# Four feature-major projections per layer in products of 512 columns instead of 256

## The chip, the cores and the metric

The kernel runs on one core of a Trainium2 chip. The metric is the device time of one execution in microseconds (us). The kernel before takes 1752.22 us (median of three runs, 1751.6 to 1752.3).

## The reference

Five stages work on x of 256 tokens by 1024 features, all in float32: two "hybrid" layers (L0, L1), then mixer_ab, cross attention, a convolutional FFN, conformer_conv, cross attention and FFN again. The change is in the hybrid layers only. Cut to what it touches:

```python
h = rms_norm(x, norm_pre)                     # 256 x 1024
proj = h @ w_in                               # sb_q, ml_q, ml_k, xa_q are 512 columns each, among others
z    = einsum(sb_q, sb_k) * d ** -0.5         # stick-breaking attention, 4 heads of 128
q_ml = silu(causal_conv(ml_q, conv_q))        # 4 taps along the tokens
k_ml = silu(causal_conv(ml_k, conv_k))
logits = einsum(xa_q, mem_k)                  # attention over the memory
```

## The kernel before

Every large product is made exactly enough for float32 out of fp32r parts: a weight w and a feature h are each split into a high and a low part, and the product is high w times high h, low w times high h, high w times low h (three passes). ScalarE writes the high parts of the weights (line 583), VectorE the low parts (line 1056), 128x1024 at a time. Such a piece is called a unit (512 KB, loaded by SyncE into a ring of 8 slots). Each engine does its splits at fixed places of its own program: `filled(name, i)` first emits the splits that `for_tile` finds due, which is up to five units beyond the one at which TensorE ends that tile, and only then waits for the tile. `past` does the same with a fixed number of units more. An instruction marked by `link` raises its engine's semaphore, and the engine waits for it before its next one.

A feature-major projection puts 512 output features on the partitions, four tiles f = 0 to 3 of 128 features by 256 tokens. `proj_F` (lines 1722 to 1752) makes them in four units of 2 k-tiles by 512 features, two tiles to a bank, with 96 matmuls of 256 columns. `proj_H` (lines 1754 to 1790) makes two tiles in two units of 4 k-tiles by 256 features. The high and the low part of h lie beside each other in `h_both`, so high w times both is one matmul of 512 columns, and a bank holds one tile: in its left half both products with high h, in its right half high w times low h. VectorE adds the halves (`both`, line 1110, one TENSOR_REDUCE of 128x512 to 128x256). `proj_W` is two `proj_H`. With `staged=True` its first half works in three passes of 256 columns, each waiting for the h tiles that it needs (`features_hi`, `features_lo`). sbk, mk and others already use `proj_W`; sbq, mlq, mlk and xaq use `proj_F`.

The eight PSUM banks go round by the written order `ORDER`: a tile takes the bank that was touched longest ago and is not held. `begin` makes TensorE wait for the mark ("free", ...) of the tile before in that bank. The scores `sbs` 0 to 3 hold their banks until `sbw`, which adds to them.

Order around the change, in each layer. TensorE: hT (transposes of h), sbq, sbk, gate columns mlif, sbv, memT, sbz, (L1: mv), scores sbs, mlq, mlk, sbw, mlv, (L0: mk), mle, mld, the mix sby, mlo, mlz, scores mls, and later xaq, the mix rty, xaz, gmy, scores xas. VectorE: low parts of h (line 1104), sums of sbk, gate rows (lines 1184 to 1203), masks of the scores (lines 1229 and 1230), the convolutions of mlq and mlk (line 1244), sblog (line 1251). ScalarE: high parts of h (line 654), memory norm, copies of sbq (line 690), logs of the scores (lines 733 to 735), first taps (line 743), exps sbw (line 751), copies of mlv (line 753), exps mld (lines 764 and 765).

Of the kernel before, what the change touches and what calls it, by code (L numbers as in the profile page):

```python
# [8 lines left out]
ACT = mybir.ActivationFunctionType  # L9
ALU = mybir.AluOpType  # L10
# [98 lines left out]
def build(nc, A, out, known):  # L109
# [5 lines left out]
    with ctx:  # L115
# [57 lines left out]
        def feat(i, n=1):  # L173
            return sec(i, n).rearrange("p (j s) -> p j s", s=S)
# [4 lines left out]
        def rows_of(i, n=2):  # L179
            return sec(i, n).rearrange("p (t n) -> p t n", t=NT)  # L180
# [26 lines left out]
        def two(*names):  # L207
            return [(n, i) for n in names for i in range(2)]

        def four(*names):  # L210
            return [(n, i) for n in names for i in range(4)]

        def pick(name, *at):
            return [(name, i) for i in at]
# [14 lines left out]
        GATES = lambda b: two(f"yT{b}") + four(f"gate{b}", f"up{b}")  # L229
        ORDER = {}  # L230
        for l in range(DEPTH):
            ORDER[f"L{l}"] = ((pick("cols", 0) if l == 0 else four("mk")) + four("hT") + two("sbq") + (pick("cols", 1) if l == 0 else []) + four("sbk") + pick("mlif", 0)
                              + two("sbv") + four("memT") + two("sbz") + (two("mv") if l else []) + four("sbs") + two("mlq", "mlk") + four("sbw") + two("mlv")
                              + (four("mk") if l == 0 else []) + pick("mle", 0) + four("mld") + two("sby", "mlo", "mlz")
                              + (two("mv", "cols2") if l == 0 else []) + four("mls") + two("rtq", "rtk") + four("mly")
                              + two("rtv", "rtz", "gmu", "gmv", "rqT", "rkT", "gmz") + four("rts")
                              + pick("wsT", 0) + two("xaq", "rty", "xaz", "gmy") + four("xas") + GATES(0) + four("xap")
                              + GATES(1) + two("xay") + GATES(2) + GATES(3) + two("yT4") + four("gate4", "up4") + pick("mgT", 0, 1) + pick("o", 0, 1) + pick("mgT", 2, 3) + pick("o", 2, 3))
            ORDER[f"X{l}"] = (pick("v", 2, 3) + four("hT", "q") + pick("q", 4, 5) + pick("s", 0, 1) + pick("q", 6, 7) + pick("p", 0, 1) + pick("s", 2, 3) + pick("oT", 0, 1)
                              + pick("p", 2, 3) + pick("o", 0, 1) + pick("oT", 2, 3) + pick("o", 2, 3))  # L240
            ORDER[f"F{l}"] = ((pick("k", 0, 1) if l == 0 else []) + four("hT") + (pick("k", 2, 3) if l == 0 else []) + four("o")
                              + [g for j in range(6) for g in four(f"g{j}", f"u{j}")])
# [43 lines left out]
        def halves(b):  # L286
            return b[:, :].rearrange("p (j s) -> p j s", j=2)
# [5 lines left out]
        def weight_order():  # L293
# [29 lines left out]
            def win(l, *at):  # L323
                for c in at:
                    col("w_in", (l,), c)
# [5 lines left out]
            for l in range(DEPTH):  # L331
                mem_k, mem_v = (lambda: halved("w_mem_kv", (l,), 0)), (lambda: col("w_mem_kv", (l,), W))
                if l:
                    mem_k()
                win(l, SBQ)
                halved("w_in", (l,), SBK)
                got.append((True, kmaj("w_in", (l,))[:, :, MLI:MLI + 2 * H]))
                win(l, SBV, SBZ)
                if l:
                    mem_v()  # L340
                win(l, MLQ, MLK, MLV)
                if l == 0:
                    mem_k()
                win(l, MLO, MLZ)
                if l == 0:
                    mem_v()
                win(l, RTQ, RTK, RTV, RTZ, GMU, GMV, GMZ)
                plain(A["gm_ws"][l].rearrange("g p q -> p g q"))
                win(l, XAQ, XAZ)
                for b in range(5):  # L350
                    win(l, GATE + b * D, GATE + b * D + W)
                    chunk("w_up", (l, b), 0)
                crossed("w_out", (l,))
# [215 lines left out]
        def _(act):  # L569
            def link(ins, *names):  # L570
                ins.then_inc(act_done, SC(*names))
                act.wait_ge(act_done, SC.n)
# [95 lines left out]
            def layer(l):  # L668
# [16 lines left out]
                if l == 0:  # L685
                    up_to(8)
                    act.wait_ge(mem_in, 16)
                    whole_norm(rows_of(6), "mem", loaded=True)
                for i in range(2):
                    copy(feat(0)[:, 2 * i:2 * i + 2, :], "sbq", i, ACT.Copy, f"sbq{i}", view=halves, scale=HD ** -0.5)  # L690
                if l == 0:
                    copy(cols[:, 8:104], "cols", 1, ACT.Copy, "cols", view=lambda b: b[:, 8:104])
                for_tile("sbk", 3)
# [41 lines left out]
                    link(nc.scalar.activation(e, e, ACT.Ln, bias=1.0), f"sbln{h}")  # L735

                def taps(n, name, s):
                    for i in range(2):
                        b = halves(filled(name, i))
                        for j in range(2):  # L740
                            ft = 2 * i + j
                            c = 52 * l + 16 + 16 * n + 12 + ft
                            link(nc.scalar.activation(feat(s)[:, ft, :], b[:, j, :], ACT.Copy, scale=cols[:, c:c + 1]),
                                 f"{name}.tap{ft}")

                taps(0, "mlq", 11)
                taps(1, "mlk", 12)
# [61 lines left out]
                for t in range(NT):  # L809
                    copy(tok(21)[:, t, :], "gmz", t, ACT.Silu, f"gmz{t}")  # L810
                head_norm("rt")
                for i in range(2):
                    copy(feat(2)[:, 2 * i:2 * i + 2, :], "xaq", i, ACT.Copy, f"xaq{i}", view=halves)
                for t in range(NT):
                    copy(tok(17)[:, t, :], "xaz", t, ACT.Silu, f"xaz{t}")
                pr = sec(15, 2)
# [224 lines left out]
        def _(dve):  # L1041
# [127 lines left out]
            def layer(l):  # L1169
# [8 lines left out]
                    all_of(feat(4), "mk", (2, 3), 2)  # L1178
                if l == 0:
                    whole_norm(rows_of(6), rows_of(6), "mem", "mem.n")  # L1180
                all_of(feat(1), "sbk", range(4), 4)
                b = filled("mlif")
                dve.wait_ge(bif_in, 4 * 16)
# [46 lines left out]
                    link(tt(e, e, con(C_LKM, TRI), ALU.mult), f"sblk{h}")  # L1230

                def conv(n, name, s):
                    for i in range(2):
                        b = halves(filled(name, i))
                        for j in range(2):
                            ft = 2 * i + j
                            dve.wait_ge(act_done, after_act(f"{name}.tap{ft | 1}"))
                            for d in range(1, 4):
                                c = 52 * l + 16 + 16 * n + 4 * (3 - d) + ft
                                y = feat(s)[:, ft, d:S]  # L1240
                                marks = [("free", name, i)] if d == 3 and j == 1 else []
                                if marks and i == 1:
                                    marks.append(name + ".conv")
                                link(stt(y, b[:, j, 0:S - d], cols[:, c:c + 1], y, ALU.mult, ALU.add), *marks)

                conv(0, "mlq", 11)
                conv(1, "mlk", 12)
# [78 lines left out]
                        link(tt(tok(20)[:, t, :], tok(20)[:, t, :], brow[:, o:o + W], op), *(["gmln"] if t and op == ALU.add else []))  # L1326
                b = quarters(filled("wsT"))
                link(tt(wsT[:, :, :], b, con(C_GMM).unsqueeze(1).to_broadcast([P, 4, P]), ALU.mult), "wsT", ("free", "wsT", 0))
                for t in range(NT):
                    b = filled("rty", t)  # L1330
                    link(nc.vector.tensor_copy(tok(22)[:, t, :], b[:, :]), ("free", "rty", t))
# [293 lines left out]
        def _(pe):  # L1625
# [219 lines left out]
            def layer(l):  # L1845
# [12 lines left out]
                norm_T()  # L1858
                if l:
                    proj_H("mk", 1, M_HL["L1"], (1,))  # L1860
                proj_F("sbq", **NORMED)
                if l == 0:
                    pe.wait_ge(rows_in, 10 * 16)
                    b = begin("cols", 1)
# [13 lines left out]
                proj_T("sbz")  # L1878
                if l:
                    proj_T("mv", src=M_HL["L1"])  # L1880
                pe.wait_ge(act_done, SC.at("sbq1"))
                pe.wait_ge(vec_done, VC.at("sbksum3"))
                for h in range(H):
                    scores("sbs", h, feat(0), feat(1))
                proj_F("mlq")
                proj_F("mlk")
                sbr = sec(13, 2)
                for h in range(H):

# [73 lines left out]
                for g in range(4):  # L1963
                    ins = nc.tensor.transpose(b[:, g, :], w[:, g, :], ident)
                used(ins, ("wsT", 0))
                proj_F("xaq")
                pe.wait_ge(vec_done, VC.at("rtsc3"))
                for t in range(NT):
                    mix("rty", t, sbr, tok(6))
# [3 lines left out]
                for t in range(NT):  # L1973
# [1 line left out]
                    for g in range(4):  # L1975
                        ins = mm(b[:, g, :], wsT[:, g, :], tok4(20)[:, t, g, :], start=True, stop=True)
                    end(ins, "gmy", t)
                pe.wait_ge(act_done, SC.at("xaq1"))
                for h in range(H):
                    b = halves(begin("xas", h))  # L1980
                    for t in range(NT):
# [292 lines left out]
```

## Time and profile before

| | |
|---|---|
| median of three runs | 1752.22 us |
| span of the profiled execution | 1750.3 us |
| TensorE busy | 1740.1 us, 99% |
| VectorE busy | 1283.1 us, 73% |
| ScalarE busy | 1024.5 us, 59% |
| matmuls | 9406 |
| share of the chain that ended last | TensorE 91%, VectorE 6% |

The profile gives the span of its execution, from the first to the last instruction, and no time beside it; the timed runs lie 1.3 to 2.0 us above the span. A busy time of TensorE counts matmuls from start to modelled end, so its pace is read better from the starts of groups in the timeline than from the mean of one.

### The profile page before, as it was taken

The page shows a single profiled execution, that of the slowest core. Times are in us where ns is not written, and L with a number is a line of the kernel's source. Part 1 is how long each engine was busy: PE and PEld are TensorE (multiplying, and loading weights), DVE is VectorE, ACT ScalarE, POOL GpSimd, SP SyncE. Part 2 cuts the span into 40 slices and gives each one's busy share as a digit, 9 for nine tenths or more (in the row PEclk, how much of TensorE's full clock was granted, in tenths as well). Part 3 has the DMA queues.
Part 4 walks back from the last instruction along what each step waited for, and adds up shares of the span by engine and source line. Part 5 has one row for each costly group of instructions (what it writes and reads, how often), then busy time and mean ns, then how long its engine had stood idle before and what let it go on. Part 6 is the DMA issues. An engine that isn't in the chain of part 4 may idle for free.

```text
span 1750.3 us, 24767 instructions
## 1 busy us (share of the span) xinstructions
PE 1740.1 (99%) x9406; PEld 1512.0 (86%) x9406; DVE 1283.1 (73%) x1714; ACT 1024.5 (59%) x1417; POOL 114.3 (7%) x186
## 2 busy tenths in 40 slices
PE   9999999999999999999999999999999999999998
PEld 8988898888889888888889988888888988888887
DVE  6966676665877586757669787688778987678775
ACT  7865566454666655644555765755556656555544
POOL 5000000000000000000000000500003360000000
PEclk9999999999999999999999999999999999999999
DMA  9656654566765566565666664456665515356663
GB/s 303 193 157 178 177 169 151 175 190 186 213 181 160 166 181 175 156 181 169 191 195 197 182 192 157 144 182 193 192 186 186 171 36 181 121 169 188 188 189 109
DMA packets 204070, 306.64 MB, mean 175 GB/s; under 512 B 12362, under 2 KB 100340, under 8 KB 203824
## 3 DMA queue, kind: packets, MB, share of 16 engines
q1 hardware_dynamic: 201056, 298.91, 56.1%
q0 software_dynamic: 2896, 6.15, 1.1%
q8 instruction: 75, 1.23, 0.3%
q14 instruction: 43, 0.35, 0.1%
HBM read 303.97 MB, written 1.05 MB: 174 GB/s over the span
## 4 chain that ended last, share of the span: by engine, by line
PE 91%; DVE 6%; ACT 1%; issue 1%; DMA 0%; DVEq 0%; ACTq 0%
PE bank L1696 52%; PE bank L1761 22%; PE bank L1728 8%; DVE bank L1573 2%; DVE weights_lo L1056 2%; PE bank L1801 1%; PE bank L1815 1%; PE bank L2093 1%; PE bank L2111 1%; PE bank L1823 1%; PE bank L1784 1%; ACT weights_hi L583 1%; PE bank L2017 0%; PE bank L1982 0%; PE bank L2065 0%
## 5 line engine op out<-in xcount | busy, mean ns | idle before, releaser
L1056 DVE TENSOR_TENSOR weights_lo<-weights_raw,weights_hi 128x1024 fp32r<-128x1024 f32 x560 | 668.9, 1233 | 248.6 <-ACT weights_hi L583 243.7
L583 ACT ACTIVATE weights_hi<-weights_raw 128x1024 fp32r<-128x1024 f32 x560 | 574.8, 1056 | 386.0 <-DMA weights_raw<-in_w_in_dram 181.3
L1696 PE MATMUL bank<-weights_hi,h_parts 128*128 128x512 f32 x1856 | 567.6, 391 | 0.4 <-DVE h_parts L1478 0.2
L1696 PEld LDWEIGHTS bank<-weights_hi,h_parts 128*128 128x128 f32 x1856 | 348.1, 188 | 73.3 <-DVE h_parts L1478 0.6
L1696 PE MATMUL bank<-weights_lo,h_parts 128*128 128x512 f32 x928 | 348.0, 390 | 0.0
L1696 PE MATMUL bank<-weights_hi,arena_parts 128*128 128x512 f32 x928 | 270.1, 391 | 0.0
L1761 PE MATMUL bank<-h_parts,weights_hi 128*128 128x512 f32 (+1 forms) x992 | 241.0, 385 | 0.5 <-DVE arena L1110 0.4
L1696 PEld LDWEIGHTS bank<-weights_lo,h_parts 128*128 128x128 f32 x928 | 174.4, 188 | 35.3
L1696 PEld LDWEIGHTS bank<-weights_hi,arena_parts 128*128 128x128 f32 x928 | 173.6, 188 | 35.4
L1761 PEld LDWEIGHTS bank<-h_parts,weights_hi 128*128 128x128 f32 x992 | 175.3, 189 | 31.8 <-DVE arena L1110 0.9
L1696 PE MATMUL bank<-weights_lo,arena_parts 128*128 128x512 f32 x464 | 158.4, 390 | 0.0
L1110 DVE TENSOR_REDUCE arena<-bank 128x256 f32<-128x512 f32 x148 | 102.1, 690 | 66.3 <-PE bank L1761 63.4
L1761 PEld LDWEIGHTS bank<-h_parts,weights_lo 128*128 128x128 f32 x992 | 134.8, 191 | 8.8
L1761 PE MATMUL bank<-h_parts,weights_lo 128*128 128x256 f32 x992 | 138.4, 283 | 0.0
L1728 PE MATMUL bank<-h_parts,weights_hi 128*128 128x256 f32 x768 | 133.7, 284 | 0.0
L1728 PEld LDWEIGHTS bank<-h_parts,weights_hi 128*128 128x128 f32 x768 | 116.3, 192 | 0.2 <-issue 0.2
L1696 PEld LDWEIGHTS bank<-weights_lo,arena_parts 128*128 128x128 f32 x464 | 87.2, 188 | 17.9
L1728 PE MATMUL bank<-h_parts,weights_lo 128*128 128x256 f32 x384 | 99.8, 284 | 0.0
L603 ACT ACTIVATE arena<-bank 128x512 f32<-128x512 f32 x140 | 83.0, 593 | 15.4 <-PE bank L1696 9.0
L1728 PEld LDWEIGHTS bank<-h_parts,weights_lo 128*128 128x128 f32 x384 | 69.7, 192 | 0.2 <-DVE weights_lo L1056 0.2
L960 ACT ACTIVATE arena<-arena,vector_columns 128x256 f32<-128x256 f32 x48 | 28.9, 602 | 64.7 <-DVE arena L1110 64.7
L541 POOL TENSOR_SCALAR arena<-constants_sb,vector_columns 128x128 f32<-128x128 f32 x76 | 35.4, 486 | 390.0 <-PE bank L1696 207.5
(326 smaller groups left out, 1667.6 us busy)
## 6 DMA issues: line engine op xcount, KB each, us to landing
weights_raw<-in_w_in_dram SPq DMA_DIRECT2D x224, 512.0 KB, 3.7
weights_raw<-in_f_w_up_dram SPq DMA_DIRECT2D x96, 512.0 KB, 3.5
weights_raw<-in_f_w_down_dram SPq DMA_DIRECT2D x48, 512.0 KB, 3.6
weights_raw<-in_w_up_dram SPq DMA_DIRECT2D x40, 512.0 KB, 3.5
weights_raw<-in_c_w_pw_dram SPq DMA_DIRECT2D x24, 512.0 KB, 3.6
weights_raw<-in_ab_w_in_dram SPq DMA_DIRECT2D x20, 512.0 KB, 3.8
weights_raw<-in_w_mem_kv_dram SPq DMA_DIRECT2D x16, 512.0 KB, 3.6
weights_raw<-in_w_out_dram SPq DMA_DIRECT2D x16, 512.0 KB, 3.6
```

The costliest lines, as they stand in the source:

```text
L541: ins = nc.gpsimd.tensor_scalar(diag(ft, d), ident, cols2[:, c:c + 1], 1.0, ALU.mult, ALU.mult)
L583: nc.scalar.activation(w_hi[:, q % SPLIT, 0:w], raw[:, n % RAW, 0:w], ACT.Copy).then_inc(hi_done, 1)
L603: link(nc.scalar.activation(dst, (view(b) if view else b[:, :]), func, **kw), ("free", name, i), *marks)
L960: link(nc.scalar.activation(c[:, f, :], feat(2)[:, f, :], ACT.Identity, scale=cols2[:, w0 + 48 + ft:w0 + 49 + ft], bias=cols2[:, b0 + ft:b ...
L1056: tt(w_lo[:, n % RAW, 0:w], raw[:, n % RAW, 0:w], w_hi[:, q % SPLIT, 0:w].bitcast(F32), ALU.subtract)\
L1110: link(nc.vector.tensor_reduce(dst, b, AX.X, ALU.add), ("free", name, f), f"{name}sum{f}")
L1573: stt(dst, feat(2, 2)[:, ft, 0:S - d], cols2[:, c:c + 1], acc[:, j, d:S], ALU.mult, ALU.add)\
L1696: return mm(bs[t][:, :], sp_[:, 2 * u + kk, t * P:(t + 1) * P], wp[:, kk, :], start=first and u == us[0] and kk == 0 and n == 0, stop=last ...
L1728: return mm(bs[i][:, j, :], wp[:, kk, f * P:(f + 1) * P], sp_[:, 2 * u + kk, :], start=first and u == us[0] and kk == 0 and n == 0 and j == 0,
L1761: return mm(out, w[n][:, kk, j * P:(j + 1) * P], sp_, start=u == 0 and kk == 0 and n == 0, stop=u == 1 and kk == 3, skip_group_check=True)
L1784: ins = mm(bs[j][:, 1, :], w[0][:, kk, j * P:(j + 1) * P], src[1][:, k, :], start=False, stop=u == 1 and kk == 3, skip_group_check=True)
L1801: ins = nc.tensor.transpose(b[:, j, t * P:(t + 1) * P], src[:, t, (2 * i + j) * P:(2 * i + j + 1) * P], ident)
```

## The change

sbq, mlq, mlk and xaq are made by `proj_W` instead of `proj_F` (sbq with `staged=True`). Their weights are loaded in halves of 256 features, each tile has its own bank, and VectorE adds the halves of the banks. For sbq ScalarE first writes the scaled left half and VectorE adds the scaled right half to it. For mlq and mlk VectorE's sums go to SBUF (`feat(s - 2)`), from where ScalarE makes the first tap and VectorE the other three. For xaq the sums go to `feat(2)` and ScalarE's copies are gone.

```diff
-ORDER: two("sbq") ... two("mlq", "mlk") ... two("xaq", "rty", "xaz", "gmy")
+ORDER: four("sbq") ... four("mlq") + four("mlk") ... four("xaq") + two("rty", "xaz", "gmy")
 # weight order
-                win(l, SBQ)
+                halved("w_in", (l,), SBQ)
...
-                win(l, MLQ, MLK, MLV)
+                halved("w_in", (l,), MLQ)
+                halved("w_in", (l,), MLK)
+                win(l, MLV)
...
-                win(l, XAQ, XAZ)
+                halved("w_in", (l,), XAQ)
+                win(l, XAZ)
 # ScalarE
-                for i in range(2):
-                    copy(feat(0)[:, 2 * i:2 * i + 2, :], "sbq", i, ACT.Copy, f"sbq{i}", view=halves, scale=HD ** -0.5)
+                for f in range(4):
+                    b = filled("sbq", f)
+                    link(nc.scalar.activation(feat(0)[:, f, :], b[:, 0:S], ACT.Copy, scale=HD ** -0.5), f"sbq.part{f}")
 def taps(n, name, s):
-                        b = halves(filled(name, i))
...
+                    for ft in range(4):
+                        for_tile(name, ft)
+                        act.wait_ge(vec_done, after_vec(f"{name}sum{ft}"))
+                        c = 52 * l + 16 + 16 * n + 12 + ft
+                        link(nc.scalar.activation(feat(s)[:, ft, :], feat(s - 2)[:, ft, :], ACT.Copy, scale=cols[:, c:c + 1]),
+                             f"{name}.tap{ft}")
...
-                for i in range(2):
-                    copy(feat(2)[:, 2 * i:2 * i + 2, :], "xaq", i, ACT.Copy, f"xaq{i}", view=halves)
 # VectorE, ahead of sbk's sums
+                for f in range(4):
+                    b = filled("sbq", f, 4)
+                    dve.wait_ge(act_done, after_act(f"sbq.part{f}"))
+                    link(stt(feat(0)[:, f, :], b[:, S:2 * S], HD ** -0.5, feat(0)[:, f, :], ALU.mult, ALU.add), ("free", "sbq", f), f"sbq{f}")
 def conv(n, name, s):
+                    all_of(feat(s - 2), name, range(4), 4)
+                    for ft in range(4):
+                        dve.wait_ge(act_done, after_act(f"{name}.tap{ft}"))
...
 # VectorE, ahead of the copies of rty
+                all_of(feat(2), "xaq", range(4), 4)
 # TensorE
-                proj_F("sbq", **NORMED)
+                proj_W("sbq", staged=True)
...
-                proj_F("mlq")
-                proj_F("mlk")
+                proj_W("mlq")
+                proj_W("mlk")
...
-                proj_F("xaq")
+                proj_W("xaq")
```

The scores now wait for VectorE's marks sbq3 and xaqsum3 instead of ScalarE's sbq1 and xaq1. By `ORDER`, the banks of mlk 0 to 3 are now those of mlq 0 to 3, and the banks of mlv 0 and 1 are those of mlk 0 and 1.

## Rows read from the trace of the kernel before

**Rows 1.** The page: span; busy us, share, instructions; TensorE's granted clock in 40 slices.

```profile
span 1750.3 us, 24767 instructions
...
PE 1740.1 (99%) x9406; PEld 1512.0 (86%) x9406; DVE 1283.1 (73%) x1714; ACT 1024.5 (59%) x1417; POOL 114.3 (7%) x186
...
PEclk9999999999999999999999999999999999999999
```

**Rows 2.** TensorE's waits: us in total, times, longest us.

```profile
PE bank L1843 <- DVE arena L1172: 1.2, 1, 1.2
PE bank L1801 <- DVE arena L1089: 0.8, 1, 0.8
```

**Rows 3.** Timeline of TensorE, layer 1: start us, length us, instruction, count.

```profile
474.62 1.12 PE L1728 MATMUL bank<-h_parts,weights_hi 128*128 128x256 f32 x8
...
486.13 2.00 PE L1761 MATMUL bank<-h_parts,weights_hi 128*128 128x512 f32 x8
...
497.31 0.28 PE L1870 MATMUL bank<-h_parts,weights_hi 128*100 128x256 f32 x1
```

**Rows 4.** Timeline of all engines, 5 to 36 us, layer 0's first projection.

```profile
9.12 1.97 ACT L654 ACTIVATE h_parts<-bank,vector_columns 128x256 fp32r<-128x256 f32 x4
...
9.72 1.19 PE L1728 MATMUL bank<-h_parts,weights_hi 128*128 128x256 f32 x8
...
14.05 0.96 ACT L654 ACTIVATE h_parts<-bank,vector_columns 128x256 fp32r<-128x256 f32 x2
...
15.85 1.00 DVE L1104 SCALAR_TENSOR_TENSOR h_parts<-bank,vector_columns,h_parts 128x256 fp32r<-128x256 f32 x2
...
21.59 0.25 PE L1865 MATMUL bank<-constants_sb,vector_rows 104*128 104x104 f32 x1
```

**Rows 5.** Groups by form, VectorE: busy us, mean ns of one, idle before.

```profile
L1110 DVE TENSOR_REDUCE arena<-bank 128x256 f32<-128x512 f32 x148 | 102.1, 690 | 66.3 <-PE bank L1761 63.4
...
L1534 DVE SCALAR_TENSOR_TENSOR arena<-arena,vector_columns 128x255 f32<-128x255 f32 x48 | 23.2, 484 | 2.0 <-DVE arena L1110 0.4
```

**Rows 6.** Timelines of VectorE, ScalarE and TensorE, layer 0, 34 to 100 us.

```profile
39.40 0.47 DVE L1184 TENSOR_SCALAR arena<-bank,gate_biases 4x256 f32<-4x256 f32 x1
...
70.07 0.56 DVE L1230 TENSOR_TENSOR arena<-arena,constants_sb 128x384 f32<-128x384 f32 x1
70.67 4.63 DVE L1056 TENSOR_TENSOR weights_lo<-weights_raw,weights_hi 128x1024 fp32r<-128x1024 f32 x4
...
45.56 1.21 ACT L603 ACTIVATE arena<-bank 128x512 f32<-128x512 f32 x2
...
68.85 0.53 ACT L735 ACTIVATE arena<-arena 128x384 f32<-128x384 f32 x1
...
60.85 0.36 PE L1728 MATMUL bank<-h_parts,weights_hi 128*128 128x256 f32 x1
```

**Rows 7.** Timelines of VectorE, ScalarE and TensorE, layer 1, 520 to 590 us.

```profile
544.74 0.56 DVE L1230 TENSOR_TENSOR arena<-arena,constants_sb 128x384 f32<-128x384 f32 x1
...
560.72 6.16 DVE L1244 SCALAR_TENSOR_TENSOR arena<-bank,vector_columns,arena 128x255 f32<-128x255 f32 x12
566.91 2.33 DVE L1251 SCALAR_TENSOR_TENSOR arena<-bank,constants_sb 128x384 f32<-128x384 f32 x4
...
544.08 3.90 ACT L583 ACTIVATE weights_hi<-weights_raw 128x1024 fp32r<-128x1024 f32 x4
...
574.02 0.58 ACT L603 ACTIVATE arena<-bank 128x512 f32<-128x512 f32 x1
...
537.17 0.36 PE L1728 MATMUL bank<-h_parts,weights_hi 128*128 128x256 f32 x1
...
560.29 0.60 PE L1893 MATMUL bank<-arena,constants_sb 128*128 128x256 f32 x2
...
563.72 0.47 PE L1696 MATMUL bank<-weights_hi,h_parts 128*128 128x512 f32 x1
...
577.54 0.39 PE L1835 MATMUL bank<-arena 128*128 128x128 f32 x2
```

More of the change, by code:

```diff
@@ L231, in build @@
         for l in range(DEPTH):
-            ORDER[f"L{l}"] = ((pick("cols", 0) if l == 0 else four("mk")) + four("hT") + two("sbq") + (pick("cols", 1) if l == 0 else []) + four("sbk") + pick("mlif", 0)
-                              + two("sbv") + four("memT") + two("sbz") + (two("mv") if l else []) + four("sbs") + two("mlq", "mlk") + four("sbw") + two("mlv")
+            ORDER[f"L{l}"] = ((pick("cols", 0) if l == 0 else four("mk")) + four("hT") + four("sbq") + (pick("cols", 1) if l == 0 else []) + four("sbk") + pick("mlif", 0)
+                              + two("sbv") + four("memT") + two("sbz") + (two("mv") if l else []) + four("sbs") + four("mlq") + four("mlk") + four("sbw") + two("mlv")
                               + (four("mk") if l == 0 else []) + pick("mle", 0) + four("mld") + two("sby", "mlo", "mlz")
@@ L236, in build @@
                               + two("rtv", "rtz", "gmu", "gmv", "rqT", "rkT", "gmz") + four("rts")
-                              + pick("wsT", 0) + two("xaq", "rty", "xaz", "gmy") + four("xas") + GATES(0) + four("xap")
+                              + pick("wsT", 0) + four("xaq") + two("rty", "xaz", "gmy") + four("xas") + GATES(0) + four("xap")
                               + GATES(1) + two("xay") + GATES(2) + GATES(3) + two("yT4") + four("gate4", "up4") + pick("mgT", 0, 1) + pick("o", 0, 1) + pick("mgT", 2, 3) + pick("o", 2, 3))
@@ L737, in taps @@
                 def taps(n, name, s):
-                    for i in range(2):
-                        b = halves(filled(name, i))
[L740 to L744, printed above, removed]
+                    for ft in range(4):
[4 more added lines that the diff above has]
+                             f"{name}.tap{ft}")
                 taps(0, "mlq", 11)
@@ L811, in layer @@
                 head_norm("rt")
-                for i in range(2):
-                    copy(feat(2)[:, 2 * i:2 * i + 2, :], "xaq", i, ACT.Copy, f"xaq{i}", view=halves)
                 for t in range(NT):
@@ L1232, in conv @@
                 def conv(n, name, s):
[L1233 to L1244, printed above, removed]
+                    all_of(feat(s - 2), name, range(4), 4)
+                    for ft in range(4):
+                        dve.wait_ge(act_done, after_act(f"{name}.tap{ft}"))
+                        for d in range(1, 4):
+                            c = 52 * l + 16 + 16 * n + 4 * (3 - d) + ft
+                            y = feat(s)[:, ft, d:S]
+                            link(stt(y, feat(s - 2)[:, ft, 0:S - d], cols[:, c:c + 1], y, ALU.mult, ALU.add),
+                                 *([name + ".conv"] if d == 3 and ft == 3 else []))
                 conv(0, "mlq", 11)
@@ L1880, in layer @@
                     proj_T("mv", src=M_HL["L1"])
-                pe.wait_ge(act_done, SC.at("sbq1"))
+                pe.wait_ge(vec_done, VC.at("sbq3"))
                 pe.wait_ge(vec_done, VC.at("sbksum3"))
@@ L1977, in layer @@
                     end(ins, "gmy", t)
-                pe.wait_ge(act_done, SC.at("xaq1"))
+                pe.wait_ge(vec_done, VC.at("xaqsum3"))
                 for h in range(H):
```

## The prediction

> **What bounds the kernel now.** I read the page's busy times first, then TensorE's waits, then timelines of the stretches that the change touches, one engine at a time, and the groups of instructions by form for the prices. TensorE is busy for 1740.1 of the span's 1750.3 us [rows 1], and its longest waits are 1.2 us, at the very start, and 0.8 [rows 2]. So each microsecond less of matmul stream is a microsecond less of time, and each new wait of TensorE is a microsecond more. The profiled execution has the span 1750.3 us; the timed runs' median is 1752.22, 1.9 us above it. I add to the span and keep the 1.9.
>
> **The stream of products.** An old projection (96 products of 256 columns) runs from 474.62 to 486.13, 11.51 us, and the form it is to take (32 products of 512 columns, 32 of 256) is already there for sbk: 486.13 to 497.31, 11.18 us [rows 3]. One changed projection is worth 0.33 us; for sbq only the second half takes the wide form, 0.165. That is 6 x 0.33 + 2 x 0.165 = 2.3 us over two layers, if nothing waits. By pace: 0.120 us per narrow product before, and 2.79 us per weight unit after against 2.88.
>
> The Trainium skill, TensorE: Matmul & The Clock Gate, section Back-to-back issue gap, gives a warm gap of N/2.4 + 2.5 ns. By it the old form is 96 x 109 ns and the new one 32 x 216 + 32 x 109, and a projection gains 0.08 us, the eight 0.6. Here a narrow product takes 120 ns, so the sum goes by the rows.
>
> **What is added and removed elsewhere.** Per layer VectorE gets 12 sums of a bank's halves at 0.69 us [rows 5] and 4 scalar_tensor_tensor of 256 columns at 0.50 [rows 4], some 10.6 us with gaps, and ScalarE loses two copies of xaq. The convolution's 12 instructions cost VectorE 6.16 us as before (they now read SBUF and not a bank; the same instruction with both operands in SBUF is 0.484 us elsewhere [rows 5], so no gain and no loss, 0.51 with the gap [rows 7]). The same 512 KB per unit is loaded, in other slices, at no cost that I can see: sbk's form arrives no later. What matters is who stands in line behind the new sums. TensorE starts a pair of tiles only when the last readers of both their banks are done; ScalarE and VectorE work in program order, with weight splits in between (0.98 and 1.15 us each, four before mlq's first tile before, now two before each pair of tiles).
>
> **Layer 0, sbq.** The staged form takes the h tiles twice as fast: its first unit wants tiles 0 to 3, its second 4 to 7. ScalarE makes 0 to 3 by 11.09 and, behind two splits, tiles 6 and 7 at 14.05 to 15.01; VectorE's low parts of these end at 16.85 [rows 4]. First unit: high pass ends 11.4, two passes of 0.96 follow, 13.4. Second: its last high tile is at 15.0, so the pass ends 15.35, the weights' low pass 16.3, then two products, a wait to 16.95 and six more: 17.7. The other two tiles take 5.59: 23.3 against 21.6 now: **+1.7 us**. In layer 1 all eight tiles are made by 475.4, h low by 476.9, no wait is left, and it gains 0.165.
>
> VectorE in layer 0 now does four instructions and waits for ScalarE's four parts of sbq, which wait for the memory norm, before sbk's sums. I make that sums from 32.85 instead of 30.71, so the gate rows start at 41.6 instead of 39.40 and ScalarE's string that begins with the sbv copies at 45.56 starts 2.2 us late; it runs without a hole to the last log of the scores at 69.38, so it arrives 2.2 late [rows 6].
>
> **The hand-over from mlq to mlk.** Scores hold four banks until sbw. Before, mlq's two and mlk's two tiles filled the other four. Now mlq takes all four, and mlk's first pair needs the banks of mlq 0 and 1, free when VectorE has summed them. VectorE comes to it after the last mask product of the scores (70.07 + 0.56) and two of the four splits that followed. Layer 0: 70.67 + 2.33 + 1.42 = 74.42, plus the 2.2: 76.6, restart 76.7. TensorE would be there at 60.85 + 1.7 + 11.18 = 73.7: a gap of 3.0 us. Where it began mlk at 72.4 (half of the 23.12 us that both took in layer 1), it now begins 4.3 late [rows 6]. Layer 1, in the old trace's times: 545.34 + 2.33 + 1.42 = 549.07 against 537.17 + 11.18 = 548.35: a gap of 0.8 with the restart at 549.15 [rows 7]. mlk's second pair is just in time in both (sums 2 and 3 end 554.5, needed 554.74).
>
> **From mlk to the mix, layer 1.** VectorE: convolution of mlq 554.5 to 560.7, two splits to 563.0, mlk's sums 0 and 1 to 564.45, two splits behind ScalarE's to 568.4, sums 2 and 3 to 569.8, convolution to 576.0, four sblog to 578.35. Before, sblog ended at 569.24 [rows 7]: 9.1 us late now, of which 5.7 are the eight sums and the rest is waiting for splits and taps in turn. TensorE: mlk ends 560.33, sbw (3.43 us) 563.77, then mlv needs mlk's banks 0 and 1: 564.55, a gap of 0.8. mlv, mle and mld end about 578.3 (mlv 11.0 us), the weights sbw3 come from ScalarE at 578.95. The second mix tile writes the bank of mlv 0, which ScalarE empties only after its exps and four splits: 578.95 + 3.93 + 0.6 = 583.5. TensorE is there at 579.95: a gap of 3.6. It began at 577.54; it now begins at 583.55, **+6.0** including two projections' 0.66. No later tile waits that I can find: mlo's banks are free by 585.1.
>
> Layer 0 has the mk projection of 11.2 us between mlv and the mix, which covers the late exps. There mlv waits for mlk's sum 1, at 89.75 + 2.2 by the same string, so mlv begins 92.05 instead of 87.40 (60.85 and the 26.55 us from mlq to mlv of layer 1): **+4.65** in all, the 1.7 of sbq and both projections in it. mk's second half needs ScalarE's split at about 107.5, 1 us before TensorE; the mix has 0.3 us to spare at mk's sum 2.
>
> **xaq.** The sums stand just before VectorE's rty copies, which wait for TensorE anyway, and xas comes the whole xaz projection of 11 us later. Hidden; -0.33 each. Without that cover the four sums would cost up to 2.8 us per layer.
>
> Sum: 4.65 - 0.33 + (-0.17 + 6.0 - 0.33) = **+9.8 us**. Span 1760.1, time **1762.0**. Bounds: if layer 0's string is late only by what TensorE itself is (1.7) 0.5 less; if a restart costs 0.3 instead of 0.1 at five places, 1 more; the splits' waits in the string, 1.5 either way.
>
> **Rivals.** (a) The new sums hide, as VectorE is idle for a quarter of the span [rows 1]: only the stream counts, 1752.2 - 2.3 = 1749.9, faster. For it: sbk, in this form, waits for nothing now. Against: sbk has a bank rotation of eight, mlk has four, and VectorE is in line behind the masks with its splits [rows 6].  Its mark is that mlk's first product follows mlq's last within 0.3 us in both layers. (b) ScalarE's lateness does not reach the mix (its splits are done while it waits, say): layer 1 loses its two gaps of 0.8 and gains 0.8, layer 0 is some 3 to 4 late: +4, 1756.2. With VectorE one split earlier at the hand-overs, as little as +2.5, 1754.7, no measurable change. (c) The gaps of 3.0 and 3.6 us let TensorE's clock fall. In this trace the granted clock is at its full level throughout [rows 1] and no wait is longer than 1.2 us [rows 2], so no row shows it; a unit of 2.79 us at 1.2 GHz instead of 2.4 would take as much again. One unit at each of the two gaps is +5.6: 1767.6. The Trainium skill, same page, section Why this matters for your kernels, asks for no gaps of that order between bursts of matmuls; by that rule (c) holds. (d) The change does not do what it says, the wide form costing as much as the narrow: 2.3 more than the forecast, 1764.3; against it stand the two rows of sbk and sbq side by side.
>
> **Chances.** Forecast with (d) 0.70 (1759 to 1765), (b) 0.14, half of it within 0.2%, (c) 0.09, (a) 0.07. A change of 0.2% (3.5 us) is about what a measurement of this kernel tells from none: faster 0.06, same 0.10, slower 0.84. The range reaches to (b) and (c): 1755.5 to 1768.
>
> **What would show it.** TensorE's list of waits gets four new entries of 0.7 to 3.7 us: at mlk's first product in both layers (for VectorE's sums), at mlv's (the same), and at the mix tile of layer 1 (for ScalarE's copy of mlv), where the long one stands. A staged sbq in layer 0 ends near 17.7 and sbk begins near 23.3. Unstaged projections of the changed kind take 11.18 us. VectorE's last sblog of layer 1 ends some 9 us later against the scores. If mlk follows mlq without a gap the forecast is wrong at its centre; if the mix tile doesn't wait, it is wrong by 3.6 us.

## The result and the profile after

The changed kernel takes 1758.93 us (median of four, 1758.83 to 1759.32), the kernel before 1752.01 beside it (1751.6 to 1752.3): 6.9 us more, ratio 1.0040 (95% interval 1.0026 to 1.0054). It is slower, and by less than the 9.8 us forecast: 1758.93 lies in the forecast's range of 1755.5 to 1768, and just below the 1759 at which its own narrower interval begins.

The page: span, busy us, granted clock.

```profile
span 1757.1 us, 24388 instructions
...
PE 1740.7 (99%) x9182; PEld 1501.2 (85%) x9182; DVE 1302.5 (74%) x1746; ACT 1023.1 (58%) x1417; POOL 116.2 (7%) x186
...
PEclk9999999999999999999999999999999999999999
```

TensorE's busy time is 0.6 us more than before [rows 1], though there is 2 us less of stream: among others, matmuls at a lower clock, of which more below, count as busy. Most of the 6.8 us of span stands in the list of TensorE's waits (us in total, times, longest), against [rows 2]:

```profile
PE bank L1837 <- ACT arena L606: 3.1, 1, 3.1
PE bank L1698 <- DVE arena L1341: 2.4, 2, 1.2
PE bank L1845 <- DVE arena L1173: 1.2, 1, 1.2
PE bank L1763 <- ACT h_parts L657: 1.0, 2, 0.5
PE bank L1803 <- DVE arena L1090: 0.8, 1, 0.8
```

Three are new: the second mix tile of layer 1 waits for ScalarE's copy of mlv (3.1), the first gate tile of each layer for the VectorE instructions that read gmy out of its bank (1.2 each), and sbq of layer 0 for its h tiles (0.5 twice).

TensorE, layer 0 (start, length): the staged sbq from 10.12, sbk from 23.73, mlq from 62.95, mlk from 74.20.

```profile
10.12 1.93 PE L1763 MATMUL bank<-h_parts,weights_hi 128*128 128x256 f32 x8 [0.48 <-ACT h_parts L657]
...
14.96 1.01 PE L1763 MATMUL bank<-h_parts,weights_hi 128*128 128x256 f32 x4 [0.52 <-ACT h_parts L657]
...
18.11 2.00 PE L1763 MATMUL bank<-h_parts,weights_hi 128*128 128x512 f32 x8
...
23.73 2.09 PE L1763 MATMUL bank<-h_parts,weights_hi 128*128 128x512 f32 x8
...
62.95 2.07 PE L1763 MATMUL bank<-h_parts,weights_hi 128*128 128x512 f32 x8
...
74.20 2.00 PE L1763 MATMUL bank<-h_parts,weights_hi 128*128 128x512 f32 x8
```

mlk begins 11.25 us after mlq, without the forecast gap. VectorE shows why: its first two sums come straight after the last mask (line 1235), and the splits of two units only after them.

```profile
71.98 0.56 DVE L1235 TENSOR_TENSOR arena<-arena,constants_sb 128x384 f32<-128x384 f32 x1
72.57 1.42 DVE L1111 TENSOR_REDUCE arena<-bank 128x256 f32<-128x512 f32 x2
74.02 2.36 DVE L1057 TENSOR_TENSOR weights_lo<-weights_raw,weights_hi 128x1024 fp32r<-128x1024 f32 x2
76.30 1.41 DVE L1111 TENSOR_REDUCE arena<-bank 128x256 f32<-128x512 f32 x2
```

ScalarE, layer 1, before the mix: it idles 8.57 us for the last sblog, makes its exps, then four splits, and only then the copy that frees the bank.

```profile
575.05 2.30 ACT L754 ACTIVATE arena<-arena 128x384 f32<-128x384 f32 x4 [8.57 <-DVE arena L1252]
577.39 3.90 ACT L586 ACTIVATE weights_hi<-weights_raw 128x1024 fp32r<-128x1024 f32 x4
581.19 0.57 ACT L606 ACTIVATE arena<-bank 128x512 f32<-128x512 f32 x1
```

TensorE there; before, a pair of matmuls (0.39 us) came every 0.22 us [rows 7]. Now, behind the wait, the matmuls soon come every 0.21 us instead of 0.11, into the first products of mlo. From 582.50 to 584.50 the granted clock is 0.50, the lower of TensorE's two levels (1.2 and 2.4 GHz); from 586.00 on it is 1.00 again. This is called the slow stretch below.

```profile
577.70 1.05 PE L1835 MATMUL bank<-arena 128*128 128x128 f32 x8
581.82 0.49 PE L1837 MATMUL bank<-arena 128*128 128x128 f32 x2 [3.07 <-ACT arena L606]
582.14 0.40 PE L1838 MATMUL bank<-arena 128*128 128x128 f32 x2
582.37 0.61 PE L1837 MATMUL bank<-arena 128*128 128x128 f32 x2
582.77 0.64 PE L1838 MATMUL bank<-arena 128*128 128x128 f32 x2
...
584.76 0.77 PE L1698 MATMUL bank<-weights_hi,h_parts 128*128 128x512 f32 x1
585.33 0.61 PE L1698 MATMUL bank<-weights_lo,h_parts 128*128 128x512 f32 x1
...
586.25 0.40 PE L1698 MATMUL bank<-weights_lo,h_parts 128*128 128x512 f32 x1
```

By stages (start to start), after against before, in us of span:

- layer 0: sbq +1.71 and its start +0.40; mlq and mlk -0.66; xaq -0.33 and the gates' wait +1.18. The sum is 2.3; 1.9 are left at layer 1's sbq (476.52 against 474.62).
- layer 1: sbq -0.16, mlq and mlk -0.66, the mix +3.07 and the slow stretch +1.6, xaq and the gates +0.85. The sum is 4.7, and with the 1.9 it is 6.6 of the 6.8.

The 1.6 are 2.94 us from 581.82 to 584.76 where full pace takes 1.81 (x1 below), and 1.49 from there to 586.25 instead of 1.01.

### The profile page after: what moved, and what is told of

Same layout as the page of the kernel before. It is cut to its first block, busy times and chain, and to the rows that moved or that the text cites. A ratio compares the mean times of both kernels' runs of the same rounds, so it can differ in the third digit from the quotient of the medians.

```text
span 1757.1 us, 24388 instructions
## 1 busy us (share of the span) xinstructions
PE 1740.7 (99%) x9182; PEld 1501.2 (85%) x9182; DVE 1302.5 (74%) x1746; ACT 1023.1 (58%) x1417; POOL 116.2 (7%) x186
## 4 chain that ended last, share of the span: by engine, by line
PE 94%; DVE 4%; issue 1%; ACT 1%; DMA 0%; SPq 0%; DVEq 0%; ACTq 0%
PE bank L1698 51%; PE bank L1763 26%; PE bank L2174 3%; PE bank L1730 3%; PE bank L2223 2%; PE bank L1803 1%; DVE weights_lo L1057 1%; PE bank L2095 1%; PE bank L2113 1%; PE bank L1817 1%; PE bank L1786 1%; PE bank L1825 1%; PE bank L2019 0%; ACT weights_hi L586 0%; PE bank L1984 0%
## 5 line engine op out<-in xcount | busy, mean ns | idle before, releaser
L1763 PE MATMUL bank<-h_parts,weights_hi 128*128 128x512 f32 (+1 forms) x1248 | 303.2, 384 | 1.5 <-ACT h_parts L657 1.0
L1763 PEld LDWEIGHTS bank<-h_parts,weights_hi 128*128 128x128 f32 x1248 | 219.8, 189 | 41.2 <-ACT h_parts L657 2.0
L1763 PEld LDWEIGHTS bank<-h_parts,weights_lo 128*128 128x128 f32 x1248 | 169.4, 190 | 11.2
L1763 PE MATMUL bank<-h_parts,weights_lo 128*128 128x256 f32 x1248 | 174.0, 282 | 0.0
L1111 DVE TENSOR_REDUCE arena<-bank 128x256 f32<-128x512 f32 x172 | 118.6, 689 | 59.4 <-PE bank L1763 55.8
L606 ACT ACTIVATE arena<-bank 128x512 f32<-128x512 f32 x132 | 78.3, 593 | 15.6 <-PE bank L1698 9.2
L1536 DVE SCALAR_TENSOR_TENSOR arena<-arena,vector_columns 128x255 f32<-128x255 f32 x96 | 46.5, 484 | 3.4
L1763 PE MATMUL bank<-arena_parts,weights_hi 128*128 128x512 f32 x192 | 48.3, 393 | 0.0
L1730 PE MATMUL bank<-h_parts,weights_hi 128*128 128x256 f32 x256 | 46.6, 284 | 0.0
L624 ACT ACTIVATE spatial_weights<-x_tokens 128x512 f32<-128x512 f32 x32 | 20.2, 632 | 42.6 <-DVE x_tokens L1168 39.3
```

The source lines that it names most:

```text
L1111: link(nc.vector.tensor_reduce(dst, b, AX.X, ALU.add), ("free", name, f), f"{name}sum{f}")
L1536: link(stt(c[:, f, d:S], sums[:, f, 0:S - d], cols2[:, cc:cc + 1], c[:, f, d:S], ALU.mult, ALU.add), *([f"conv{j}"] if d == 2 and f == 3 e ...
L1730: return mm(bs[i][:, j, :], wp[:, kk, f * P:(f + 1) * P], sp_[:, 2 * u + kk, :], start=first and u == us[0] and kk == 0 and n == 0 and j == 0,
L1763: return mm(out, w[n][:, kk, j * P:(j + 1) * P], sp_, start=u == 0 and kk == 0 and n == 0, stop=u == 1 and kk == 3, skip_group_check=True)
```

## The experiments

All times are medians, in us; "span" is that of the profiled execution. The kernel before took 1752.17 beside x1 to x4, 1752.04 beside y1 to y4 and 1752.11 beside z1 to z3. All experiments but x4 and z2 start from the changed kernel, and all are compared with the kernel before. Where a diff is shown, it is cut to the lines that matter.

**x1: layer 0's sbq narrow again.**

```diff
-                proj_W("sbq", staged=True)
+                if l == 0: proj_F("sbq", **NORMED)
+                else:      proj_W("sbq", staged=True)
```

> The changed kernel with sbq of layer 0 alone back in products of 256 columns (its weights, copies and bank order too). Theory: the staged wide form costs TensorE 2.1 us there (it starts 0.4 later, behind the first weights, and waits for the h tiles), and everything after it is late by just that; the mlq projection of layer 0 should start at 60.9 instead of 62.95, and the time fall by 2.1, from 1758.9 to 1756.8. Rival: the lateness is swallowed later by a wait that both kernels have, and the time stays within 0.5 of 1758.9.

Measured: 1759.34 (1756.98 to 1760.22), span 1755.2, ratio to before 1.0042 (1.0027 to 1.0056). mlq of layer 0 starts at 60.89 and layer 1's first mix tile 2.04 earlier than in the changed kernel (575.66 against 577.70): this part of the theory holds. The time did not fall, for two reasons. First, a new wait far downstream, behind cross attention:

```profile
1126.33 2.06 PE L1768 MATMUL bank<-arena_parts,weights_hi 128*128 128x512 f32 x8 [1.06 <-DVE x_tokens L1173]
```

With two tiles fewer in the written order nearly every later tile sits in another bank (worked out from the written order, all tiles of mixer_ab and of the cross attention after it are shifted by 6 of the 8 banks), and here a product meets a bank whose residual is not yet read. The changed kernel has eight tiles more per layer than the one before, 16 in all, so its rotation after the layers is the old one. Second, the profiled execution was the fastest of five by 2.2 us. In it the same gap at the mix was followed by no slow stretch at all, and the other four lie above the changed kernel's 1758.93. They have no trace, so that a slow stretch explains them is not shown:

```profile
579.79 0.49 PE L1842 MATMUL bank<-arena 128*128 128x128 f32 x2 [3.08 <-ACT arena L609]
580.12 0.39 PE L1843 MATMUL bank<-arena 128*128 128x128 f32 x2
580.34 0.39 PE L1842 MATMUL bank<-arena 128*128 128x128 f32 x2
```

**x2: xaq narrow again**, with ScalarE's copies, `proj_F("xaq")`.

> The changed kernel with xaq back in products of 256 columns and ScalarE's copies in both layers. Theory: the sums of xaq in VectorE's line, with two splits that come with them, delay the gmy products by 2.3 us and give TensorE its waits of 1.2 us at the first gate tiles of both layers, against 0.33 won per projection; without them 2 x (1.2 - 0.33) = 1.7 less, 1757.2. Rival: the waits at the gates come from lateness further up (the strings of VectorE after mlq and mlk), they stay, and only the 0.66 us of stream come back: 1759.6.

Measured: 1759.32 (1756.28 to 1759.48), span 1754.5, ratio 1.0036 (1.0022 to 1.0049). Both waits at the gates are gone, so they do come from xaq's sums; by the median nothing is won. This kernel too has another bank rotation (mixer_ab shifted by 4 banks), and meets no new wait above 0.4 us there. Again the profiled execution was the fastest, without a slow stretch after its gap of 3.08; 3.2 us lie between it and the slowest. These medians cannot carry a part of 1.7 us; the starts in the traces can.

**x3: in layer 1 the copies of mlv ahead of the four splits.**

```diff
-                    copy(values_one(t)[:, :, 0:HD], "mlv", t, ACT.Copy, view=quarters)
+                    b = quarters(filled("mlv", t, 0 if l else None))
+                    link(nc.scalar.activation(values_one(t)[:, :, 0:HD], b, ACT.Copy), ("free", "mlv", t))
```

> The changed kernel, but in layer 1 ScalarE copies both tiles of mlv right behind its exps and makes the four weight splits after them. Theory: the second mix tile no longer waits 3.07 us, and the clock that fell behind that gap (the mix matmuls at 0.21 to 0.22 us each instead of 0.11, for about 1.7 us in all) stays up: 4.7 less, 1754.2, with every mix matmul at 0.11. Rival 1: the slow stretch has another cause and stays: 3.1 less, 1755.8. Rival 2: the four splits, now 1.7 us later, make mlo's units late, and TensorE waits at mlo for 1 us or more: 1755.2 or above.

Measured: 1759.40 (1758.63 to 1760.11), span 1758.3. The theory and rival 1 failed; rival 2 had the place and the size (TensorE waits at mlo for over 1 us) but not the cause. The mix no longer waits, but mlo's second tile needs mle's bank, and ScalarE empties it only behind the same four splits (579.37 to 583.17):

```profile
583.63 0.77 PE L1699 MATMUL bank<-weights_hi,h_parts 128*128 128x512 f32 x1 [2.87 <-ACT statistics L763]
584.19 0.63 PE L1699 MATMUL bank<-weights_lo,h_parts 128*128 128x512 f32 x1
584.62 1.06 PE L1699 MATMUL bank<-weights_hi,h_parts 128*128 128x512 f32 x2
```

A wait is not mended by moving one of several readers past the block. Here the slow stretch is longest: from mlo's first product to its sixth product with low weights 6.61 us instead of 3.74 (x1), 2.9 lost.

**x4: mlq and mlk alone wide** (sbq and xaq as before).

> The kernel before with only mlq and mlk in the wide form (sbq and xaq as before). Theory: the parts add up. mlq and mlk win 4 x 0.33 = 1.3 us of stream and pay the wait at layer 1's second mix tile, 3.1, and the slow clock behind it, 1.7: 3.4 to 3.5 more than before, 1755.5; the hand-over from mlq to mlk has no gap in either layer, since VectorE sums the first two tiles straight after the masks of the scores. Rival: the long wait needs sbq's lateness in VectorE's line as well; then it is below 1 us and the time is at or below that of before, 1751 to 1752.

Measured: 1756.74 (1754.63 to 1758.45), ratio 1.0026 (1.0015 to 1.0037), span 1754.7. The median is 1.2 above the theory's 1755.5, which lies within the spread; the profiled execution also began its first product 1.0 late (10.70 against 9.72). The wait at the mix is 3.09 without any change to sbq, and no gap follows mlq.

```profile
580.31 0.80 PE L1842 MATMUL bank<-arena 128*128 128x128 f32 x2 [3.09 <-ACT arena L608]
```

**y1: the four splits ahead of the exps, layer 1**, into ScalarE's idle 8.57 us.

```diff
                 taps(1, "mlk", 12)
+                if l:
+                    for_tile("mlv", 0)
```

> The changed kernel, but in layer 1 ScalarE makes the four weight splits that stand between its exps and the copies of mlv ahead of the exps, in the 8.6 us in which it waits for the last sblog. Theory: no wait is left at the mix nor at mlo, since the copies of mlv and mle follow the exps at once; TensorE loses neither the 3.07 us nor the slow stretch behind it: a span of 1757.1 - 3.07 - 1.7 = 1752.3, a time of 1754.2, and its runs lie as close together as those of the kernel before (within 0.8 us; the kernels with the gap spread by 1.5 to 3.8), because it is only behind that gap that the clock sometimes falls. Rival: the splits wait for weights or for TensorE's units, the exps start late, and the gap moves to the first mix tile: 2 to 3 us there and no gain.

Measured: 1754.42 (1753.92 to 1756.17), ratio 1.0015 (1.0006 to 1.0024), span 1752.6; theory 1754.2 and 1752.3. The mix has no wait and no slow stretch:

```profile
574.11 1.06 ACT L586 ACTIVATE weights_hi<-weights_raw 128x1024 fp32r<-128x1024 f32 x1 [1.55 <-DMA weights_raw<-in_w_in_dram]
575.15 2.37 ACT L756 ACTIVATE arena<-arena 128x384 f32<-128x384 f32 x4
577.55 0.60 ACT L606 ACTIVATE arena<-bank 128x512 f32<-128x512 f32 x1
```

These two lines give back 4.5 of the 6.9 us. The spread, 2.3 us over 11 runs, is not as small as I expected: nine lie within 1.0, two above.

**y2: xaq's sums in the head norm**, two in each of the places where VectorE waits for ScalarE there (behind the marks `.cen` and `.ms`).

> The changed kernel with VectorE's four sums of xaq moved behind the copies of rty, into the two stretches of the head norm in which VectorE waits for ScalarE (1.2 us and 0.65 us in layer 0): two sums in each. Theory: the copies of rty stand 5 us earlier in VectorE's line, the gmy products end at least 2 us earlier, and the waits of 1.18 us at the first gate tiles of both layers go: 2.4 less span; the gap before the mix stays with its chance of a slow clock, so the time is 1756.5, 1755 to 1758. Rival: the two weight splits that VectorE makes before the third sum come with the sums wherever they stand, the gmy products are still over 1 us late, and at most half of the waits goes: 1757.7 or above.

Measured: 1759.27, ratio 1.0041 (1.0028 to 1.0055); the gates wait 1.09 instead of 1.18. The theory was wrong; the rival's numbers came. In layer 0 the copies of rty end only 1.0 us earlier (250.49 against 251.45) and not 5, as they wait for TensorE, and the sums (2 x 1.42) are 1.0 longer than the two waits that they fill (1.20 and 0.65). So the products of gmy still start at 264.68 (264.50 in the changed kernel), behind four splits:

```profile
258.87 1.23 DVE L1302 TENSOR_TENSOR arena<-arena 128x1024 f32<-128x1024 f32 x1
260.13 4.63 DVE L1057 TENSOR_TENSOR weights_lo<-weights_raw,weights_hi 128x1024 fp32r<-128x1024 f32 x4
264.68 3.04 DVE L1344 SCALAR_TENSOR_TENSOR arena<-bank,vector_columns,arena 128x128 f32<-128x128 f32 x8
```

In the kernel before the same eight products end at 265.26 and TensorE's gate product follows 0.1 us later:

```profile
262.21 3.05 DVE L1339 SCALAR_TENSOR_TENSOR arena<-bank,vector_columns,arena 128x128 f32<-128x128 f32 x8
265.36 0.47 PE L1696 MATMUL bank<-weights_hi,h_parts 128*128 128x512 f32 x1
```

In the changed kernel TensorE restarts 0.1 us behind VectorE too (267.55 and 267.65), so the kernel before had no slack here: it already waited some 0.2 us, which no list of waits shows. (The scores xas and the first gate product behind them lie 4.46 us apart, 260.90 to 265.36; in z1 below, where VectorE is done at 263.24, 4.25.) Any 1 us more on that string of VectorE is 1 us of time.

**y3: the sums where the prediction had them.**

```diff
-                    all_of(feat(s - 2), name, range(4), 4)
+                    all_of(feat(s - 2), name, range(4))
```

> The changed kernel with the sums of mlq and mlk placed as the prediction took them: VectorE makes all weight splits that are due (for_tile) before each pair of sums, instead of only the four units of past. Theory: this order is the whole reason that the forecast gaps at mlk did not come. Now they do: in layer 0 VectorE is at mlq's first sum at 72.5 + 2.3 and done with the second at 76.3, TensorE ready at 74.15: a gap of 2.2 us; in layer 1 one of 0.7. The span grows by about 2.9, the time to 1761.8, with a chance of a slow clock behind the first gap on top. Rival: the splits of that moment are not ready for VectorE before the sums anyway, or the restart is set by something else, and the time stays at 1758.9.

Measured: 1766.65 (1765.70 to 1766.97), ratio 1.0083 (1.0069 to 1.0097), span 1763.9. The gaps come: 1.97 at mlk in layer 0 (2.2 expected), 0.55 in layer 1 (0.7), then 0.50 at mlv and 0.60 at the first mix tile. Behind the first one the clock fell too (granted 0.64 from 76.00 to 78.00, 0.51 from 78.00 to 80.00), which made it dearer than I said:

```profile
75.88 3.16 PE L1763 MATMUL bank<-h_parts,weights_hi 128*128 128x512 f32 x8 [1.97 <-DVE arena L1111]
78.84 1.63 PE L1763 MATMUL bank<-h_parts,weights_lo 128*128 128x256 f32 x8
80.30 2.00 PE L1763 MATMUL bank<-h_parts,weights_hi 128*128 128x512 f32 x8
```

One unit took 4.42 us (75.88 to 80.30) where it takes 2.79. The span is 3.9 above the theory's (1757.1 + 2.9): 1.6 are this unit and 1.1 the waits at mlv and the mix; the rest is not accounted for.

**y4: all parts that pay, first try.** Two entries in the order that no product uses, behind layer 0's sbq, were to restore the later rotation.

> The parts that pay, with the waits mended: wide form for mlq, mlk and xaq in both layers and for sbq in layer 1 only (layer 0's sbq is narrow, and two entries that no product uses keep the bank rotation of all later stages as in the changed kernel), the splits ahead of the exps in layer 1, the sums of xaq in the waits of the head norm. Theory: what is left is the stream, 4 x 0.33 + 2 x 0.33 + 0.17 = 2.15 us less than before, none of the new waits: a span of 1748.2, a time of 1749.9, ratio 0.9988, with a spread as small as that of before. Rival: one of the mended waits comes back in part (mix 1 to 3 us, gates 1 us each) and eats the gain: 1751 to 1754.

Measured: 1757.53, ratio 1.0031 (1.0019 to 1.0042). Wrong by 7.6. Some 4.5 of it are my padding, 2.94 of wait and 1.6 of lower clock behind it (from 30.60 to the end of sbk at 37.80, 7.20 us instead of 5.59): sbk's last tile now takes the bank of sbq 0, which ScalarE empties only after the memory norm and two splits, from 29.92 us on (in the wide form its first part goes at 27.09). The waits at the gates (1.08, 1.09) stayed, as in y2. The mix had neither a wait nor a slow stretch.

```profile
30.60 2.52 PE L1777 MATMUL bank<-h_parts,weights_hi 128*128 128x512 f32 x8 [2.94 <-issue]
32.92 1.91 PE L1777 MATMUL bank<-h_parts,weights_lo 128*128 128x256 f32 x8
```

**z1: the same, mended.** The padding stands at the head of mixer_ab (`AB`), and VectorE makes two splits instead of four before gmy (diff against y4).

```diff
-                    b = filled("gmy", t)
+                    b = filled("gmy", t, 2)
...
-        ORDER["AB"] = (four("k", "hT", "pu", "rec") ...
+        ORDER["AB"] = (two("pad") + four("k", "hT", "pu", "rec") ...
```

> mlq, mlk and xaq wide in both layers, sbq wide in layer 1 only; splits ahead of the exps in layer 1; sums of xaq behind the copies of rty, in the waits of the head norm, and VectorE makes two weight splits instead of four before the gmy products (the other two after them). The two bank entries that no product uses now stand at the head of the stage after the layers, so that layer 0 keeps the rotation of the run with narrow sbq, and the later stages that of the changed kernel. Theory: no new wait is left (none at the second half of sbk, none of 1.06 us behind cross attention, none at the gates), and the stream gives 4 x 0.33 + 2 x 0.33 + 0.17 = 2.15 us: span 1748.2, time 1749.9. Rival: the two splits behind the gmy products come too late for the first gate units or delay the maxima of the xa scores, TensorE waits 1 us in each layer: 1752.

Measured: 1750.33 (1749.71 to 1751.35), ratio 0.9990 (0.9981 to 0.9999), span 1748.7. It is 8.6 us below the changed kernel and 1.8 below the one before; that second interval ends just under 1. Waits over 0.6 us are only those of [rows 2]; neither the gates nor the products behind cross attention wait. VectorE at gmy now waits for TensorE itself:

```profile
257.44 1.23 DVE L1313 TENSOR_TENSOR arena<-arena 128x1024 f32<-128x1024 f32 x1
260.19 3.05 DVE L1355 SCALAR_TENSOR_TENSOR arena<-bank,vector_columns,arena 128x128 f32<-128x128 f32 x8 [1.53 <-PE bank L1998]
263.28 3.50 DVE L1068 TENSOR_TENSOR weights_lo<-weights_raw,weights_hi 128x1024 fp32r<-128x1024 f32 x3
```

**z2: mlq and mlk alone, with y1's line.**

> The kernel before with mlq and mlk alone in the wide form, and the splits ahead of the exps in layer 1. Theory: the wide form itself pays, 4 x 0.33 = 1.3 us less than before, as soon as the copy of mlv is not behind the splits: span 1749.0, time 1750.7, with the small spread of the kernel before. Rival: VectorE's eight sums per layer cost TensorE something elsewhere (they stand before the scores' products and the convolutions), and the time is that of before, 1752.

Measured: 1751.50 (1750.82 to 1752.34), ratio 0.9996 (0.9987 to 1.0005), span 1749.0. The profiled span is the theory's; by the times, 0.6 below the kernel before, a gain of 1.3 cannot be told from none.

**z3: the whole change with both mends.**

> The changed kernel with all four projections wide in both layers and both mends (splits ahead of the exps in layer 1; xaq's sums in the head norm and two instead of four splits before the gmy products). Theory: against the run with the splits ahead of the exps (span 1752.6, time 1754.4) the two waits of 1.18 us at the gates go: span 1750.2, time 1752.1, and what keeps it from the 1749.7 that the stream alone would give is the staged sbq of layer 0. Rival: the lateness at the gates is set by something else than VectorE's four splits before the gmy products; the waits stay, 1754.4.

Measured: 1751.87 (1751.28 to 1752.44), ratio 0.9999 (0.9990 to 1.0008), span 1750.1; theory 1752.1 and 1750.2. The gates do not wait, so it was the four splits ahead of gmy together with the sums that made them late: without the sums (x2) four splits do no harm, and moving the sums alone (y2) does not help. Fewer splits with the sums in their old place was not run.

## Why the prediction came out as it did

The direction was right and the time lies in the range. The sum, 9.8 against 6.9, came near by luck: it has too much in one place and too little in two. By the prediction's own sign (mlk follows mlq without a gap) it was wrong at its centre. Of its four new waits one came, the long one at the mix.

- *The stream.* Right. The projections take 11.17 to 11.25 us, the staged one 11.35 (476.52 to 487.87, layer 1); z1's span gains 1.6 of the 2.15 expected; it waits some 0.5 for VectorE's sums at mlk in layer 0, and its first product is 0.25 later. Rival (d) falls.
- *sbq in layer 0*, +1.7: from its first product to sbk's, 13.61 us (10.12 to 23.73) against 11.90 (9.72 [rows 4] to 21.62, below): +1.71. The further 0.4 are when the first weights land: over the thirteen traces of this study ScalarE's first split begins anywhere from 8.05 to 9.14 us, in either form.

```profile
21.62 2.09 PE L1761 MATMUL bank<-h_parts,weights_hi 128*128 128x512 f32 x8
```

- *The hand-over*, 3.0 and 0.8 us, and mlv's gaps behind it: the step that failed. "VectorE comes to it after the last mask product of the scores (70.07 + 0.56) and two of the four splits that followed." The code calls the sums with `past(..., 4)`, and those four units were already split; only `for_tile` would have asked for two more. y3 makes just this order and gets the gaps at mlk (1.97 and 0.55), so the arithmetic was right in the main and the reading of one argument wrong. (Its 549.07 should read 549.09, and its 554.5 for the end of mlq's sums has no working: they end at 552.22, which is 550.3 in the old trace's times.) The same reading made the string behind it too long: the last sblog ends at 576.73 instead of 569.24 [rows 7], 5.6 us later once the 1.9 of layer 0 are taken off, where I had 9.1. The 5.6 are the eight sums; the 3.5 of waiting for splits and taps did not come, and with them not the wait of the first mix tile for its weights.
- *The second mix tile*, 3.6: right in place and cause, 3.07 in size. y1 takes it away by moving what ScalarE does ahead of it.
- *The clock*, rival (c) with 0.09: a part of it came. Behind the 3.07 us gap about 1.6 us were lost, 1.3 to 2.9 behind such gaps in x3, x4, y2, y3 and y4, none in x1 and x2. I had priced it as 2.8 us at each of two gaps; it costs 0 to 2.9 at one.
- *xaq*, -0.33 per layer as "hidden": wrong, +0.85. I had looked at who waits for the sums and at VectorE's wait for rty, and not at what follows in its line. The norm, the splits and gmy had no slack (y2).

Rival (a) showed the mark that I had named for it (mlk follows mlq at once, in both layers) and was wrong all the same: one place is no mark for a claim on all. Against the forecast some 7 us of waits are missing (3.65 in layer 0, 3.45 up to layer 1's second mix tile) and 4 are there that I had not counted (2.4 at the gates, 1.6 of clock), with 0.4 of later start: the errors cancel, and that of the sum, 2.9, is smaller than its parts.

## What to carry to other kernels

When TensorE is at 99%, price a change by every string of VectorE and ScalarE that ends in a bank, with its slack in the trace (where a product starts 0.1 us behind the last reader of its bank there is none, though no wait is listed), and for the order of the splits read which helper call asks for them with which number. A block of splits moved into an idle stretch of its engine (y1, two lines) gave 4.5 us, twice what all the wide products are worth. Changing the number of tiles in a rotating order moves every later stage's banks: keep the count, or restore it where nothing is tight.

## What the chip showed that I had not expected

Gaps of equal length cost unequally. After a gap of 3.08 us TensorE ran on at full pace in two traces (x1, x2); after 3.07 and 3.09 it fell to its lower level, 1.2 GHz (the changed kernel; x4 and y2). It also fell after 2.87 (x3), 2.94 (y4) and 3.25 (y3). What decides it is open. The time lost to the lower clock, against the full pace of x1 or of the same unit, was:

| run, gap before | us lost |
|---|---|
| x1 and x2, 3.08 | 0 |
| x4, 3.09 | 1.3 |
| y2, 3.09 | 1.4 |
| y3, 3.25 at the mix | 1.5 |
| the changed kernel, 3.07 | 1.6 |
| y4, 2.94 | 1.6 |
| y3, 1.97 at mlk | 1.6 |
| x3, 2.87 | 2.9 |

Nine us from just after the first mix tile began, the changed kernel and then x1: busy us and instructions of PE (TensorE), PEld, DVE (VectorE), ACT (ScalarE) and POOL, then the granted clock, DMA share, GB/s.

```profile
578.00:587.00 9.00, 5.93 (x31) 5.32 (x30) 5.92 (x6) 8.56 (x19) 0.00 (x0) 0.81 0.10 39
```

```profile
576.00:585.00 9.00, 5.92 (x38) 5.16 (x37) 5.92 (x6) 8.57 (x19) 0.00 (x0) 1.00 0.11 39
```

Busy time is alike to 0.01 us and the clock is not, so a busy time cannot show it. After gaps of 1.2 us no trace here shows a fall, after 1.97 (y3) one does. The Trainium skill, TensorE: Matmul & The Clock Gate, section Why this matters for your kernels, sets the gap to avoid higher than these 1.97 us; here the measurement decides. Over their runs the kernels with a gap of about 2 us or more have a mean granted clock of 0.996 to 0.999, those without (y1, z1 to z3, before) 0.999 or 1.000. That the clock makes the whole spread is not shown: y1 has no gap and two of its eleven runs are 1 to 2 us above the rest.
